# A hybrid DeltaNet, GLA and mixture-of-experts layer on one core: six edits to the order of work around the projection chunks and the first expert pair

## The reference

```python
h = _rmsnorm(x, norm_mix)
z = h @ w_in                      # 2048 x 11,328 columns, split into 13 pieces
# mixer A: gated DeltaNet, 8 heads of 128: causal conv of 4 taps on q, k, v, SiLU, l2 norm,
#   chunked WY form: (I + strict lower triangle)^-1 by a triangular solve
# mixer B: GLA, 4 heads, per-channel decay, chunked
x = x + (sigmoid(mix_a) * (oa @ w_oa) + sigmoid(mix_b) * (ob @ w_ob)) @ w_out
h2 = _rmsnorm(x, norm_ffn)
# 4 groups x 8 experts: top group, then top 2 experts in it
x = x + sum(gate * ((silu(h2 @ w1[e]) * (h2 @ w3[e])) @ w2[e]))
return _rmsnorm(x, norm_final)
```

## Time and profile before

| | |
|---|---|
| three executions | 1803.4, 5274.58 and 1797.27 us, median 1803.4 |
| profiled execution | 1797.45 us, its span 1795.7 us |
| PE busy | 1726.4 us, 96% of the span |
| transfers | 537.41 MB, mean 299 GB/s |
| granted clock of PE, mean | 0.99 |

### The profile page before, as it was taken

How to read it: one execution, slowest core, us unless ns; L and a number is a source line. 1 busy time by engine, 2 the same in 40 slices (tenths; PEclk the granted TensorE clock), 3 DMA queues, 4 the chain that set the end, 5 groups by cost and what they waited for, 6 DMA issues and landing times.

```text
span 1795.7 us, 20998 instructions
## 1 busy us (share of the span) xinstructions
PE 1726.4 (96%) x8774; PEld 1104.3 (61%) x8774; DVE 675.6 (38%) x740; ACT 444.1 (25%) x483; POOL 169.6 (9%) x223
## 2 busy tenths in 40 slices
PE   9999999999999999999999999999999999999996
PEld 7888878888788888888544434443444443443342
DVE  5357767455744645543222202221122112220222
ACT  6344455325523433333100000000000000000002
POOL 4000042310051100000000000000000000000001
PEclk9999999999999999999999999999999999999999
DMA  8454535423533455658999999999999999999997
GB/s 262 145 168 161 164 118 187 141 94 118 171 111 105 137 188 187 225 174 321 369 419 429 427 428 429 428 429 429 428 429 428 429 428 428 428 429 428 428 425 298
DMA packets 95323, 537.41 MB, mean 299 GB/s; under 512 B 5836, under 2 KB 5900, under 8 KB 70044
## 3 DMA queue, kind: packets, MB, share of 16 engines
q1 hardware_dynamic: 94672, 535.85, 75.4%
q0 software_dynamic: 592, 0.69, 0.3%
HBM read 534.42 MB, written 2.10 MB: 299 GB/s over the span
## 4 chain that ended last, share of the span: by engine, by line
PE 72%; DMA 22%; DVE 2%; ACT 2%; issue 1%; POOL 0%; SPq 0%; DVEq 0%; ACTq 0%; POOLq 0%
DMA arena<-in_w 22%; PE psum L1994 13%; PE psum L1532 12%; PE psum L1534 12%; PE psum L1533 12%; PE psum L2021 9%; PE psum L1915 4%; PE psum L1754 1%; PE psum L1746 1%; PE psum L2039 1%; PE psum L2038 1%; PE psum L1646 1%; DVE w_lo L1044 1%; PE psum L1956 1%; PE psum L1757 0%
## 5 line engine op out<-in xcount | busy, mean ns | idle before, releaser
L1994 PE MATMUL psum<-arena 128*64 128x512 f32 x2048 | 458.8, 605 | 39.2 <-DMA arena<-in_w 38.5
L1994 PEld LDWEIGHTS psum<-arena 128*64 128x64 f32 x2048 | 148.1, 139 | 338.9 <-issue 288.0
L1044 DVE TENSOR_TENSOR w_lo<-arena,w_hi 128x2048 fp32r<-128x2048 f32 x119 | 273.2, 2298 | 194.1 <-ACT w_hi L711 184.1
L1532 PE MATMUL psum<-w_hi,hT_hi 128*128 128x512 f32 x824 | 332.1, 403 | 0.1
L1534 PE MATMUL psum<-w_hi,hT_lo 128*128 128x512 f32 x824 | 327.6, 398 | 0.0
L1533 PE MATMUL psum<-w_lo,hT_hi 128*128 128x512 f32 x824 | 327.6, 398 | 0.0
L711 ACT ACTIVATE w_hi<-arena 128x2048 fp32r<-128x2048 f32 x119 | 227.5, 1914 | 258.8 <-PE psum L1534 249.1
L2021 PE MATMUL psum<-arena 128*64 128x512 f32 x960 | 210.6, 594 | 3.4 <-DMA arena<-in_w 3.4
L1534 PEld LDWEIGHTS psum<-w_hi,hT_lo 128*128 128x128 f32 x824 | 155.8, 189 | 37.9
L1532 PEld LDWEIGHTS psum<-w_hi,hT_hi 128*128 128x128 f32 x824 | 156.1, 189 | 36.6 <-issue 0.9
L1533 PEld LDWEIGHTS psum<-w_lo,hT_hi 128*128 128x128 f32 x824 | 156.2, 190 | 35.7
(11 more groups left out here) (365 smaller groups left out, 1409.0 us busy)
## 6 DMA issues: line engine op xcount, KB each, us to landing
arena<-in_w SPq DMA_DIRECT2D x184, 2048.0 KB, 26.4
arena<-in_w_in SPq DMA_DIRECT2D x87, 1024.0 KB, 5.0
arena<-in_w_out SPq DMA_DIRECT2D x16, 1024.0 KB, 5.1
arena<-in_w SPq DMA_DIRECT2D x14, 1024.0 KB, 20.9
arena<-in_w_oa SPq DMA_DIRECT2D x8, 1024.0 KB, 5.0
arena<-in_w_ob SPq DMA_DIRECT2D x8, 1024.0 KB, 5.0
arena<-in_x SPq DMA_DIRECT2D x4, 1024.0 KB, 7.6
arena<-in_w SPq DMA_DIRECT2D x4, 512.0 KB, 15.7
```

The lines of the kernel that those rows point to most:

```text
L1044: tt(w_lo[x % RING_A], ringA[:, x % RING_A, :], w_hi[x % NSPLIT].bitcast(F32), ALU.subtract)\
L1532: mm(m_banks[m], lhs[0][:, k0 + k, ms], wh[:, cs], start=(start and k == 0), stop=False)
L1994: i = mm(bank(w)[e * CAP:(e + 1) * CAP, :], xeT[:, k, e * CAP:(e + 1) * CAP], src[e][:, (k % 8) * CB:(k % 8 + 1) * CB], start=(k == 0), st ...
```

## The change

1. **Start.** Chunk 0 and chunk 1 are multiplied with the products that need only `w_hi` first, and those with `w_lo` last, behind a wait of their own.
2. **Fillers.** One chunk moves from behind `blrT` to behind `smallT`. In each head group one moves from behind `gcb` (9 to 8, 8 to 7) to behind `PT` (1 to 2, 0 to 1).
3. **Convolution.** ACT no longer calls `before` ahead of `zqT`, DVE none ahead of `zkT` and `obT0`; ahead of `zvT` ACT still does. The two exponentials move ahead of the first tanh, the two squares ahead of the third tanh; SiLU of q and k is done inside the loop over taps instead of behind it.
4. **Norm factor.** POOL squares its factor ahead of the wait for the sums, so that two fewer dependent operations stand behind it.
5. **First pair.** w2 of the first pair is loaded in four pieces of 2 MB (both experts), each as soon as half a slot is free, where before the last two came as one piece of 4 MB behind the release of slots 2 and 3. PE waits for each piece.
6. **Clock.** 36 instead of 30 idle transposes stand ahead of the ranks, and 6 new ones ahead of the first gather.

```diff
 SPANS = [
-    {"small": 1, "smallT": 0, "cw": 1, "blrT": 2, "gc": 1, "gkT": 4, "bkT": 2, "lv_eye": 2, "lv1": 2, "lv2": 1,
+    {"small": 1, "smallT": 1, "cw": 1, "blrT": 1, "gc": 1, "gkT": 4, "bkT": 2, "lv_eye": 2, "lv1": 2, "lv2": 1,
      "lv4": 2, "lv8": 1, "lv16": 2, "lv32": 1, "lv64": 2, "kd": 1, "bo1": 3},
 ] + [
     {f"{k}.0": v for k, v in
-     {"gcb": 9, "ssq": 2, "vtok": 1, "khT": 1, "PT": 1, "dU2": 1, "dU4": 1, "dU8": 1, "dU16": 1, "dU32": 1,
+     {"gcb": 8, "ssq": 2, "vtok": 1, "khT": 1, "PT": 2, "dU2": 1, "dU4": 1, "dU8": 1, "dU16": 1, "dU32": 1,
       "dU64": 1, "Y1": 1, "o": 3}.items()},
     {f"{k}.1": v for k, v in
-     {"gcb": 8, "ssq": 1, "vtok": 1, "khT": 1, "PT": 0, "dU2": 1, "dU4": 1, "dU8": 1, "dU16": 1, "dU32": 1,
+     {"gcb": 7, "ssq": 1, "vtok": 1, "khT": 1, "PT": 1, "dU2": 1, "dU4": 1, "dU8": 1, "dU16": 1, "dU32": 1,
       "dU64": 1, "Y1": 1, "o": 2}.items()},
 ]
@@ SP
-            for half in range(2):
+            for t, (freed, name) in enumerate(((("first_part", 2), "part_in"), (("slotM_free", RING_M + 2), "slotM0"),
+                                               (("first_part", 3), "w2_third"), (("slotM_free", RING_M + 4), "slotM1"))):
+                wait(sp, freed)
                 for e in range(2):
...
-            load_pair(0, 0, 0, RING_M + 2, PER_PAIR)
+                    sp.dma_start(ringM[2 * (t // 2) + e][:, t % 2 * D:(t % 2 + 1) * D], w2_v[e, :, t * D:(t + 1) * D])\
+                        .then_inc(sem(name), 16)
@@ POOL
+                link(nc.gpsimd.tensor_scalar(rqk[:, 0:8], rqk[:, 0:8], QSCALE, None, ALU.mult))
+                link(nc.gpsimd.tensor_tensor(rmf[:, 8:16], rqk[:, 0:8], rqk[:, 0:8], ALU.mult))
                 wait(pool, ("a_ms", g + 1))
-                link(nc.gpsimd.tensor_scalar(rqk[:, 0:8], rqk[:, 0:8], QSCALE, None, ALU.mult))
-                link(nc.gpsimd.tensor_tensor(rms[:, 0:8], rms[:, 0:8], rqk[:, 0:8], ALU.mult))
-                link(nc.gpsimd.tensor_tensor(rms[:, 0:8], rms[:, 0:8], rqk[:, 0:8], ALU.mult))
+                link(nc.gpsimd.tensor_tensor(rms[:, 0:8], rms[:, 0:8], rmf[:, 8:16], ALU.mult))
@@ ACT
                 for i, w in ((0, "zqT"), (2, "zvT")):
-                    result(w + s)
+                    if i:
+                        sp_.before(w + s)
+                    wait(act, full(w + s))
...
-                for i in range(3):
-                    sp_.before("ssq" + s, most=2 if i else 3)
-                    act.wait_ge(sem("conv"), 3 * g + i + 1)
-                    nc.scalar.activation(T_[f"zT{i}"][:, 0:1024], c[i], ACT.Tanh, scale=0.5).then_inc(sem("tconv"), 1)
                 wait(act, ("Dn", g + 1))
                 nc.scalar.activation(T_["Dm"], T_["Dm"], ACT.Exp, scale=-1.0).then_inc(sem("expD"), 1)
                 wait(act, ("DTn", g + 1))
                 nc.scalar.activation(T_["DT"], T_["DT"], ACT.Exp).then_inc(sem("expDT"), 1)
-                for i in range(2):
-                    act.wait_ge(sem("silu"), 3 * g + i + 1)
-                    nc.scalar.activation(T_[f"zT{i}"][:, 0:1024], c[i], ACT.Square).then_inc(sem("sq"), 1)
+                for i, most in enumerate((3, 2, 1)):
+                    sp_.before("ssq" + s, most=most)
+                    if i == 2:
+                        for j in range(2):
+                            act.wait_ge(sem("silu"), 3 * g + j + 1)
+                            nc.scalar.activation(T_[f"zT{j}"][:, 0:1024], c[j], ACT.Square).then_inc(sem("sq"), 1)
+                        sp_.before("ssq" + s, most=1)
+                    act.wait_ge(sem("conv"), 3 * g + i + 1)
+                    nc.scalar.activation(T_[f"zT{i}"][:, 0:1024], c[i], ACT.Tanh, scale=0.5).then_inc(sem("tconv"), 1)
@@ DVE
-                if i:
-                    wait(dve, full(f"obT{i}"))
-                else:
-                    result(f"obT{i}")
+                wait(dve, full(f"obT{i}"))
...
-                result("zkT" + s)
+                wait(dve, full("zkT" + s))
...
+                def silu(w):
+                    dve.wait_ge(sem("tconv"), 3 * g + w + 1)
+                    stt(c[w], T_[f"zT{w}"][:, 0:1024], 1.0, c[w], ALU.add, ALU.mult).then_inc(sem("silu"), 1)
...
+                        if w and k == 1:
+                            silu(w - 1)
                     i.then_inc(sem("conv"), 1)
...
-                for w in range(3):
-                    dve.wait_ge(sem("tconv"), 3 * g + w + 1)
-                    stt(c[w], T_[f"zT{w}"][:, 0:1024], 1.0, c[w], ALU.add, ALU.mult).then_inc(sem("silu"), 1)
+                silu(2)
@@ PE
...
+                    for k in ks:
+                        cs = slice(k * CB, (k + 1) * CB)
+                        mm(bank(m), hTh[:, k, ms], w_hi[0][:, cs], start=(k == 0), stop=False)
+                        mm(bank(m), hTl[:, k, ms], w_hi[0][:, cs], start=False, stop=False)
                     if m == 0:
                         wait(pe, ("w_lo", 1) if half else ("first_half", 2))
...
+                for wait_for, lhs, w in ((("w_hi", 2), hTh, w_hi[1]), (None, hTl, w_hi[1]), (("w_lo", 2), hTh, w_lo[1])):
...
-            keep_running(30)
+            keep_running(36)
...
-                        if first and w == 0 and q == 0:
+                        if first and w == 0 and q % 2 == 0:
                             i.then_inc(sem("first_part"), 1)
...
-                if first:
-                    wait(pe, ("part_in", 48))
                 for t in range(FT):
-                    if t % 2 == 0:
+                    if first:
+                        wait(pe, (("part_in", 48), ("slotM0", 64), ("w2_third", 32), ("slotM1", 64))[t])
+                        src = ringM[t // 2 * 2:t // 2 * 2 + 2]
+                    elif t % 2 == 0:
                         src = arrived(8 + t)
...
+            keep_running(6)
             wait(pe, ("first_sel", 1))
```

More of the change, by code:

```diff
@@ L1579, in _ @@
                     wait(pe, ("hTl", 2 * x + 2))
-                project(x)
+                if x > 1:
+                    project(x)
+                    continue
+                for wait_for, lhs, w in ((("w_hi", 2), hTh, w_hi[1]), (None, hTl, w_hi[1]), (("w_lo", 2), hTh, w_lo[1])):
+                    if wait_for:
+                        wait(pe, wait_for)
+                    for m in range(NM):
+                        for k in range(CT):
+                            i = mm(bank(m), lhs[:, CT + k, m * P:(m + 1) * P], w[:, k * CB:(k + 1) * CB], start=False,
+                                   stop=False)
+                i.then_inc(sem("chunk"), 1)
             wait(pe, ("small_split", 2))
```

15 lines of the change are left out of this document (5 added, 10 removed).

## The result

The changed kernel is slower. Over six executions its median is 1810.28 us (1805.9 to 1812.07), against 1798.08 us for the kernel before on the same chip; the ratio is 1.0057, 95% interval 1.0039 to 1.0075. The prediction was 1794.7 us with a range of 1786 to 1802: the sign is wrong and the time lies outside the range. Its profiled execution took 1810.27 us (span 1808.5, mean clock 0.985), so the two profiled executions, which differ by 12.8 us, stand for the medians (12.2 apart).

The account below looks back on a forecast made before the run. Transfers bound the experts; ahead of them PE sets the pace. From the profiled 1797.45 us, gains against losses of 4.8 and 2.5 in the first head group summed to -2.75, so 1794.7 us; range 1786 to 1802.

Parts of the forecast that it names:

- Second head group, start: Second group's start: no wait for v, gaps of 0.78 and 0.42 go, one cut late; gain 0.45 us.
- The first group's start: PE's zvT waits for ACT's evacuation of v: 4.8 us lost, plus 2.5 for the low clock behind it.
- The clock at `ssq`: Second group's ssq: the wait of 1.49 us mostly goes (gain 1.3), and with it the low clock (gain 3.2).
- The fillers: Moved chunks cover gaps: 0.65 us gained ahead of blrT; gap of 0.75 ahead of Y1 goes, within a gain of 1.2.
- The start: First chunks: PE begins with products needing only the high parts, so chunk 1 comes earlier; gain 1.15 us.
- The first pair: First expert pair: w2 pieces in earlier and PE's clock kept; gain 2.1 us, or 0.6 without the clock.
- POOL beside DVE: Convolution: POOL's three operations, moved some 35 us ahead, cost DVE perhaps 0.5 us over the three.
- the first rival: Second group's squares late, PE waits at ssq; DVE loses 3.5 us, low clock returns: 1801.1 us; chance 20%.
- My case that ends on the slow side: The case of late squares at the second group's ssq, slower than before: 1801.1 us; chance 20%.
- rival 4: First expert pair gives nothing: clock falls as before, transfers find their next hole at 888: 1796.5 us; chance 15%.
- the new wait: First head group, ahead of zvT: PE waits for v, 4.8 us, with 2.5 for the clock.

Follow-up runs that it names:

- run 6: Changed kernel with ACT's cuts ahead of its drains again in the first head group only, still late in the second: 1800.99 us, ratio 1.0008.
- run 1: Changed kernel with ACT's cuts and evacuation again ahead of the drain of zqT in both head groups: 1791.75 us, ratio 0.995.
- run 9: Kernel before with all edits of the first expert pair alone (w2 in four pieces, 6 and 6 further transposes): 1796.23 us, ratio 0.9985.
- run 10: Kernel before with the 6 and 6 further transposes alone, w2 as before: 1798.0 us, ratio 0.9989.
- run 5: Changed kernel with the numbers of filler chunks as before (smallT, blrT, gcb, PT): 1809.46 us.
- run 11: Kernel of run 1 with the filler chunk of smallT moved back to blrT: 1792.88 us.
- run 4: Kernel before with only the drain edits: ACT drains zqT, DVE drains obT0 and zkT, without their next cuts ahead: 1817.39 us, ratio 1.0103.
- run 8: Kernel before with the 16 one-column products of ssq mixed with wide products of the next chunk: 1800.14 us.

## Why the prediction was wrong

**The step that failed: "Second head group, start".** I wrote "v was evacuated long before, so no such wait" and booked -0.45. It cost 8.96 us in the trace, and 9.2 by the medians of runs 6 and 1 (10.4 by their ratios). I had walked ACT's queue for what PE waits on in the first group (v), found this absent in the second, and stopped. The other users of ACT's high cuts are DVE's low cuts, and DVE makes two of them ahead of its drain of `oaT`. A removed wait of ACT was in truth a cut moved behind a drain, and I followed it to one of its readers only. What could have told me is the order of the instructions: DVE's two cuts stand directly ahead of the drain, and ACT's cuts that they need stand behind its drain of `zqT`.

**The first group's start was right**: the wait of 6.50, the evacuation as its releaser, `zvT` at 260.85 where I had worked out 261.1, and the whole step with the clock +7.23 against +7.3. The medians of run 6 and of the changed kernel put it at 9.3, their ratios at 8.8; the 2 us between are within what single executions differ by, as the next point shows.

**The clock at `ssq` was read from one execution.** I booked -3.2 for the second group, as if idle time and clock went together, and nothing for the first. In the changed kernel the wait of 1.49 went as forecast (squares done at 503.3, `ssq` at 504.89), but a low stretch stayed, 1.71. In the first group 3.42 appeared with no idle time. Runs 9 and 10 compute the same as the kernel before up to 850 us, in the same order, and are repeats of it: their clock losses are 1.70 and 3.42 at the first `ssq`, 3.41 and 5.12 at the second, where the profiled execution had 0 and 3.42. Their first gathers start at 859.23 and 861.43, not at 856.74. So the execution I summed from was the best of three by 2.5 to 4.7 us, and a term of 3.2 read from it was within its chance. The +3.48 of the table is thus not shown to be an effect of the change.

**The fillers.** At `smallT` the gain of 0.65 was repaid by a new gap of 0.95 (runs 5 and 11): the chunk moved from behind `blrT` had given DVE the time for its next low cut. I had asked what covers the gap and not what the moved chunk covered. At `PT` the gap of 0.75 went as forecast; at `oaT` 0.46 went and 0.35 came at the chunk behind.

**The start** was right (-1.05 against -1.15).

**The first pair was right in sum and wrong in its parts**: -2.25 against -2.1. Up to pair 1 the profiled gain is 1.6, all of it clock, where I had 1.5 for the clock. W2 in four pieces gave nothing there, where I had let it count for 0.6. The other 0.65 came behind pair 1 and is within what the same code differs by (935.97 to 939.20), so that the sum agrees is luck.

**POOL beside DVE.** I took 0.5 us. In run 1 DVE lost 1.48 on its cut and 2.13 on its taps (3.3 together in the changed kernel), and POOL 2.1 on L608. Both had an instruction under way from 455.96 to 461.97, 6.0 us, and the losses come to 5.7: they took turns, each waiting for the instruction of the other that had begun before its own. DVE's cut began at 455.96 and POOL's first product ended at 457.58; L608 began at 457.53 and the cut ended at 459.73; the taps began at 459.64 and L608 ended at 461.97. These are 1.6, 2.2 and 2.3 us, beside losses of 1.48, 2.1 and 2.13. That is what the Trainium skill says (SBUF — State Buffer, on the shared port pair): an exclusive lock that goes to whichever instruction starts first, and under which the other blocks fully. The trace agrees. I had set it aside because mostly POOL waited in the earlier trace rows, but either side can be the one that waits. So DVE lost what the first rival assumed (3.5). The end of that rival did not come all the same: the squares were ready 1.5 us ahead of PE, since PE itself was later. Tap 0 ended 3.8 us after the start of the covering chunks in the changed kernel, where I had walked 8.3.

**The rivals.** None had both waits. My case that ends on the slow side was priced at 1801, since I had only one engine's lateness in it. The range was too narrow above: it allowed for one wait from item 3, and an edit of several drains on two engines can make two. Two slips of arithmetic change nothing in this: the low clock at the second `ssq` was read as 3.3 and booked as 3.2, and rival 4, which drops a term of 2.1, ends at 1796.8 and not at 1796.5.

Run 1 is the forecast without the new wait: 7.3 less, which makes 10.05 us under the profiled time of before. Measured were 7.8 under the median of before (1799.58 less 1791.75). The 2.2 that are short are less than the interval of that ratio (about 4 us to either side) can tell. The terms that did not come are known all the same: the filler's 0.65, and the clock at `ssq`, 3.2 booked as gone of which nothing went (clock loss 3.41 in that run).

## What to carry to other kernels

When a step is moved behind a wait on one engine, list every engine that reads what the step makes, and for each of them what stands behind that read in its queue; the wait that costs most may be on an engine that was not edited. A filler that is moved uncovers what it covered. And a low clock or a gap at one place of one profiled execution is a sample: before a term of some 3 us rests on it, look at the same place in other executions of the same code.

## What the runs showed of the hardware

Up to 1000 us, every stretch of low clock in these profiles cost 1.7, 3.4 or 5.1 us. Nearly all lie at the same places (behind a long wait, behind `ssq`, at the first gathers); one in run 9 does not (1.71 at 13 to 18). Their size varies: behind the wait of 8.70 us it was 5.12 in the changed kernel and 3.42 in run 6, and at the first `ssq` 0 to 3.42 over the same code. At the first gathers the code without the further transposes had a loss of 1.7 in two profiles (before, run 4) and none in a third (run 8); the code with them had none in eleven. The Trainium skill (TensorE: Matmul & The Clock Gate, on the HAM clock gate) says that the gate's window runs on its own and does not start anew with the kernel, so that the point at which the clock changes varies from run to run. The repeats agree that it varies: at the first `ssq` the clock was low from 314 to 318 in run 9 and from 312 to 320 in run 10, and at no time in the kernel before.

DVE and POOL hold each other up in both directions: in run 1 DVE needed 7.5 us for a cut and four taps that take 4.0 alone, and POOL 6.8 for two products of 2.4 each. Started 35 us later, the same products left DVE's cut and taps at 2.29 and 1.67.

A hole in the transfers at the beginning of a stage that the transfers bound (175 GB/s for 5 us) cost nothing that can be measured: pair 1 started 63.4 us after the first gather with it and without.
